# Mask copies and half picks behind each weight rounding in the recurrent heads

## The reference

```python
score = jnp.einsum('bqh,bqhs->bqs', wi, jax.nn.relu(dots)).astype(jnp.float32)
score = jnp.where(causal[None], score, -jnp.inf)
_, idx = lax.top_k(score, topk)
```

```python
A = jnp.einsum('bthk,bshk,btshk->bhts', qc, kc, decay)      # decay = exp(G[t] - G[s]) for s <= t
o_intra = jnp.einsum('bhts,bshv->bthv', A, vc)
new_state = jnp.exp(G_last)[..., None] * state + jnp.einsum('bshk,bshv->bhkv', k_dec, vc)
```

## Time and profile before

| | us |
|---|---|
| timed executions | 3150.56, 3150.81, 3156.08 |
| profiled execution | 3153.85 |
| its span, first to last instruction | 3152.1 |
| the four heads in it (step 0 of head 0 to the norm sum of head 3) | 600.4 to 784.1 |
| mean granted TensorE clock | 0.973 of full |

### The profile page before, as it was taken

The page is one execution under the profiler, slowest core; times in us unless marked ns, Lnnn a source line. Parts: engine busy times, 40 slices in busy tenths (PEclk is TensorE's granted clock), DMA queues, the critical chain, the costliest instruction groups (busy, mean ns, idle before and its releaser), DMA issues.

```text
span 3152.1 us, 37108 instructions
## 1 busy us (share of the span) xinstructions
PE 2947.3 (94%) x12850; PEld 2239.9 (71%) x12858; DVE 1462.5 (46%) x2332; ACT 932.3 (30%) x1629; POOL 1242.4 (39%) x587
## 2 busy tenths in 40 slices
PE   6899998998998999997999899999879999899999
PEld 2688875776665788875766688877657767688787
DVE  7211225887356211237266555524745443455426
ACT  2211003243442211013255233302335551233202
POOL 0455443333134555443422355544321113455544
PEclk9999998999999999998999899999989999999999
DMA  4222231221112222321222122232211112222232
GB/s 157 79 94 93 87 100 62 74 67 55 56 37 87 80 93 93 99 88 60 89 83 64 54 93 94 92 95 93 77 40 37 38 34 74 75 95 95 89 94 98
DMA packets 78617, 249.53 MB, mean 79 GB/s; under 512 B 9073, under 2 KB 15729, under 8 KB 78385
## 3 DMA queue, kind: packets, MB, share of 16 engines
q1 hardware_dynamic: 64800, 229.74, 22.9%
q10 hardware_dynamic: 13712, 18.44, 1.8%
HBM read 238.57 MB, written 9.44 MB: 79 GB/s over the span
## 4 chain that ended last, share of the span: by engine, by line
PE 81%; DVE 10%; ACT 4%; issue 3%; POOL 1%; DMA 1%; ACTq 0%; DVEq 0%; SPq 0%; POOLq 0%
PE ps L300 22%; PE ps L302 22%; PE ps L301 22%; PE ps L3059 1%; PE ps L3102 1%; PE ps L3080 1%; PE ps L3081 1%; DVE tmp L489 1%; DVE tmp L1064 1%; DVE y_ple L1062 1%; PE ps L2582 1%; PE ps L2567 1%; PE ps L1243 1%; PE ps L1876 1%; DVE h L698 1%
## 5 line engine op out<-in xcount | busy, mean ns | idle before, releaser
L294 POOL TENSOR_TENSOR w_lo<-raw,w_hi 128x1024 fp32r<-128x1024 f32 (+1 forms) x438 | 1041.9, 2379 | 1703.4 <-DVE w_hi L287 1703.4
L300 PE MATMUL ps<-xh,w_hi 128*128 128x512 f32 x2152 | 880.6, 409 | 49.4 <-DVE xl L481 20.1
L287 DVE CAST w_hi<-raw 128x1024 fp32r<-128x1024 f32 (+1 forms) x438 | 331.7, 758 | 1132.4 <-PE ps L302 1086.1
L301 PE MATMUL ps<-xl,w_hi 128*128 128x512 f32 x2152 | 856.8, 398 | 0.0
L302 PE MATMUL ps<-xh,w_lo 128*128 128x512 f32 x2152 | 856.1, 398 | 0.0
L300 PEld LDWEIGHTS ps<-xh,w_hi 128*128 128x128 f32 x2152 | 407.3, 189 | 185.2 <-issue 49.2
L302 PEld LDWEIGHTS ps<-xh,w_lo 128*128 128x128 f32 x2152 | 407.6, 189 | 100.5
L301 PEld LDWEIGHTS ps<-xl,w_hi 128*128 128x128 f32 x2152 | 408.5, 190 | 98.5 <-issue 6.5
L300 PE MATMUL ps<-ah,w_hi 128*128 128x512 f32 x704 | 279.6, 397 | 6.8 <-POOL w_lo L294 6.8
L302 PE MATMUL ps<-ah,w_lo 128*128 128x512 f32 x704 | 279.3, 397 | 0.0
L301 PE MATMUL ps<-al,w_hi 128*128 128x512 f32 x704 | 279.1, 396 | 0.0
(11 more groups left out here) (396 smaller groups left out, 3896.7 us busy)
## 6 DMA issues: line engine op xcount, KB each, us to landing
raw<-in_ffn_up SPq DMA_DIRECT2D x90, 512.0 KB, 3.7
raw<-in_conv_up SPq DMA_DIRECT2D x88, 512.0 KB, 3.6
raw<-in_ffn_down SPq DMA_DIRECT2D x32, 512.0 KB, 3.5
raw<-in_conv_down SPq DMA_DIRECT2D x32, 512.0 KB, 3.5
raw<-in_merge SPq DMA_DIRECT2D x24, 512.0 KB, 3.6
raw<-in_ple_gate SPq DMA_DIRECT2D x24, 512.0 KB, 3.6
raw<-in_diff SPq DMA_DIRECT2D x24, 512.0 KB, 3.6
raw<-in_mla SPq DMA_DIRECT2D x20, 512.0 KB, 3.6
```

What stands on the lines that cost most here:

```text
L287: dve.tensor_copy(self.w_hi[s][:, 0:n], self.raw[r][:, 0:n]).then_inc(self.sem["slot_hi"], 1)
L294: pool.tensor_tensor(self.w_lo[s][:, 0:n], self.raw[r][:, 0:n], self.w_hi[s][:, 0:n].bitcast(F32), ALU.subtract).then_inc(self.sem["slot_s ...
L300: pe.matmul(out, wh, xh, start=start, stop=False)
L301: pe.matmul(out, wh, xl, start=False, stop=False)
```

## The change

Only the order of VectorE's instructions in the heads changes; every instruction is still there, and the other engines' programs are the same. Where a level has a rounding, its mask copy stands behind the rounding and no longer ahead of it; where it has none, the copy keeps its place. The picks are cut in two (`largest`: the three MAX8; `mark`: the three MATCH_REPLACE8), and the 22 halves are dealt in turn to eight places of a head: behind the mask copies of the levels 0, 2, 3, 4, 5, 6 and 7, and behind the rounding at S. The heads 0 and 1 take 8 halves each and head 2 takes 6; `masks` follows the last.

```diff
@@ -1562,12 +1562,26 @@
             own = self.part(b)[:, b * P:(b + 1) * P]
             dve.tensor_tensor(own, own, k.causal_b, ALU.add).then_inc(k.sem["topk_masked"], 1)
 
+    def half_pick(self, dve, q, part):
+
+        if part == 0:
+            self.largest(dve, q)
+        else:
+            self.mark(dve, q)
+
     def pick(self, dve, q):
+        self.largest(dve, q)
+        self.mark(dve, q)
+
+    def largest(self, dve, q):
         k = self.k
         dve.wait_ge(*(self.on("topk_replace", 3 * q - 1) if q else self.on("topk_masked", 2)))
         k.carry(dve)
         for b in range(1, NB):
             dve.max(k.top8[:, b - 1, :], self.part(b)).then_inc(k.sem["topk_max"], 1)
+
+    def mark(self, dve, q):
+        k = self.k
         dve.wait_ge(*self.on("topk_max", 3 * q + 2))
         k.carry(dve)
         for b in range(1, NB):
@@ -1725,17 +1739,26 @@
         self.scans(dve, 0)
         self.diff(dve, 0, 1)
         k.round_hi(dve, self.w, 0, 15)
+        halves = iter([(q, part) for q in picks for part in range(2)])
+
+        def half_pick():
+            q, part = next(halves, (None, None))
+            if q is not None:
+                self.half_pick(dve, q, part)
+                if (q, part) == (self.PICKS - 1, 1):
+                    self.masks(dve)
+
         for h in range(self.HEADS):
             self.round_at(dve, h, "V")
             self.diff(dve, h, 2)
             self.product(dve, h, 1)
+            self.round_at(dve, h, 0)
             self.a_out(dve, h, 0)
-            self.round_at(dve, h, 0)
+            half_pick()
             for l in range(2, LEVELS + 1):
                 if l < LEVELS:
                     self.diff(dve, h, l + 1)
                 self.product(dve, h, l)
-                self.a_out(dve, h, l - 1)
                 if l == 3:
                     self.to_end(dve, h)
                 if l == 7:
@@ -1743,30 +1766,23 @@
                     self.round_at(dve, h, "KV")
                 else:
                     self.round_at(dve, h, l - 1)
-                if l in (2, 4, 6):
-                    q = next(picks, None)
-                    if q is not None:
-                        self.pick(dve, q)
-                        if q == self.PICKS - 1:
-                            self.masks(dve)
+                self.a_out(dve, h, l - 1)
+                if l >= 3:
+                    half_pick()
             self.carried(dve, h)
             if h + 1 < self.HEADS:
                 self.forget(dve, h + 1)
+            self.round_at(dve, h, LEVELS)
             self.a_out(dve, h, LEVELS)
-            self.round_at(dve, h, LEVELS)
+            half_pick()
             if h + 1 < self.HEADS:
                 self.scans(dve, h + 1)
                 self.diff(dve, h + 1, 1)
             self.round_at(dve, h, "O")
-            if h + 1 < self.HEADS:
-                q = next(picks, None)
-                if q is not None:
-                    self.pick(dve, q)
-                    if q == self.PICKS - 1:
-                        self.masks(dve)
             self.normed_out(dve, h)
             self.round_at(dve, h, "S")
-        assert next(picks, None) is None
+            half_pick()
+        assert next(halves, None) is None
 
     def gpsimd(self, pool):
         k = self.k
```

## The result

| | runs | median, us | lowest to highest |
|---|---|---|---|
| before | 10 | 3154.21 | 3150.56 to 3156.83 |
| changed | 10 | 3160.56 | 3157.84 to 3164.45 |

The ratio is 1.0021, 95% interval 1.0012 to 1.0029: the change costs 6.4 us by the medians, 4 to 9 by the interval. Forecast were +5.9 us, 3158.2 us, slower more likely than not. Of the 2.4 us between 3158.2 and 3160.56, 1.9 are the base: the kernel before came out at 3154.21 over ten runs, where four had given 3152.3.

What follows compares the result with a forecast made beforehand. TensorE, busy in 94% of the span, was taken as the bound, so its waits decide. The terms 3.7 + 2.2 - 0.5 + 0.5 = +5.9 us on 3152.3 gave 3158.2 us, range 3152 to 3163.

Steps and rivals of the forecast that it cites:

- Part 1: Heads 0 to 2: roundings followed by copies and halves; levels 2, 4 late 1.09, level 6 0.77; gains 0.58 us a head.
- Part 2: Step 7 of heads 0 to 2: the level 7 mask copy behind its rounding delays the output, 1.80 us a head.
- Part 3: Heads 1 and 2: GpSimd's output_low holds VectorE's subtractions, so level 4 starts 1.10 us later, twice: +2.2 us.
- Part 4: Head 3: level 1 waits less, -0.5 us; blocked first subtractions at levels 4 and 6 cost +0.5 us.
- The rival in which VectorE keeps the ports: Heads 1 and 2: VectorE keeps the shared ports, output_low never gets between; +3.7 us in all, chance 0.22.
- The clock: Head 3's level 1 may lose its clock fall, -1.5 us; waits at level 4 and output may bring up to +4.5.
- 14.8 us is about all the stage could ever give back: In the four heads, level matmuls wait for VectorE's hx 12 times, 14.8 us, taken as about the stage's whole possible gain.

Runs made afterwards that it cites:

- copies-ahead kernel: Changed kernel with all mask copies ahead of the roundings, only the picks in halves; +1.8 us, ratio 1.0007 against the kernel before.
- level 7 copy first: Changed kernel with the mask copy of level 7 ahead of its rounding again; +5.1 us, ratio 1.0015 against the kernel before.
- level 7 copy only: Kernel before with only the mask copy of level 7 moved behind its rounding, whole picks kept; +4.9 us, ratio 1.0016 against the kernel before.
- the first experiment: Changed kernel with the level 7 mask copy back ahead of the rounding at step 7; +5.1 us, ratio 1.0015 against the kernel before.
- the last two kernels: Changed kernel, level 7 copy ahead of its rounding, every level prepared one level ahead, output_low later or kept; 3136.72 and 3138.41 us, ratios 0.9944 and 0.9947 against before.

## Why the prediction was right

**Head by head.** From step 0 of one head to step 0 of the next, the kernel before takes 48.44, 48.43 and 45.65 us and the changed one 49.66, 50.70 and 47.92: +1.22, +2.27 and +2.27. Parts 1 to 3 have 1.80 - 0.58 = 1.22 for head 0 and 1.22 + 1.10 = 2.32 for the heads 1 and 2. From step 0 of head 3 to the logits it is 46.95 and 45.33; with the fall of the clock in the first put at 1.6, nothing is left, as part 4 has it. So the terms came one by one, not only their sum.

**Part 1, the roundings followed by copies and halves: right.** The waits came as worked out, 0.94 at level 2, 0.95 at level 4 of head 0, 0.61 to 0.63 at level 6, none at levels 3 and 5. The copies-ahead kernel shows that behind a rounding with a half GpSimd's `w_lo` alone sets the time of the next subtractions.

**Part 2, the level 7 copy: right.** 1.49, 1.49 and 1.50 us of wait; alone it costs 4.8 to 4.9 us, where 3 x 1.80 less 0.5 was worked out.

**Part 3, output_low: right.** 2.02 at level 4 in heads 1 and 2 against 0.95 in head 0, gone when it is moved. The rival in which VectorE keeps the ports fell: the `w_lo` of the earlier trace rows that took 3.51 has no like in the changed kernel, where those in the heads take 2.35 to 2.52. Why four VectorE instructions went ahead of GpSimd in that row stays open; I made no run on it. All six such rows of the kernel before (3.51 or 3.52) stand behind roundings at steps 2 and 4 that had not waited for TensorE, but the rounding at S in the earlier trace rows (743.23) had not waited either and its `w_lo` took 2.46, so that alone is not it. The rule of the Trainium skill that the prediction cites ("SBUF — State Buffer", the section on the two separate sides: an exclusive lock) agrees with the changed kernel's rows, where the two subtractions took 0.66 and 1.48 beside GpSimd's two instructions; it does not account for the six rows of 3.51.

**Part 4, head 3: right.** Its level 1 waits 3.02 for 3.51, its levels 4 and 6 wait 0.94 and 1.68 for 0.71 and 1.46, as worked out. ScalarE shows what lies behind the 3.02. Before, the norm's step (L1432) stood behind the next head's decay (L1394), which waited for VectorE's subtraction; in the changed kernel the decay is done early and the norm's step waits for TensorE's sum:

```profile
739.93 0.63 ACT L1394 ACTIVATE hdiff<-hdiff 128x512 f32<-128x512 f32 x1 [3.14 <-DVE hdiff L1625]
740.47 0.67 ACT L1432 ACTIVATE sq<-ps,consts 128x512 f32<-128x512 f32 x1
```

```profile
743.10 0.63 ACT L1394 ACTIVATE hdiff<-hdiff 128x512 f32<-128x512 f32 x1 [1.33 <-DVE hdiff L1639]
744.82 0.69 ACT L1432 ACTIVATE sq<-ps,consts 128x512 f32<-128x512 f32 x1 [1.08 <-PE ps L1281]
```

So the first part of the output's lateness is taken up by a path that ended later anyway, and the rest goes on to the norm, the rounding at S and level 1. In the experiments level 1 waits 3.0 even where the level 7 copy is ahead of its rounding. There the output of head 2 still waits 0.25 or 1.38, because the key masks now stand ahead of the copy. With 0.25, the first of the two paths still ends last: from level 7 of head 2 to level 1 of head 3 "level 7 copy first" takes 19.52 us, to the hundredth what the kernel before takes, so that wait of 0.25 costs nothing and only moves TensorE's idle time. With 1.5 it takes 20.78, in the changed kernel as in "level 7 copy only". I had left out that wait when I expected 3.5 in the first experiment.

**The clock.** In the profile the fall behind the 3.5 us wait is gone: level 1 to level 2 takes 755.72 - 751.94 = 3.78 where the earlier trace rows have 5.36. So the stage grew by 4.1 only, 5.7 with the fall put back. By the counts above this trace is the exception: behind the same wait of 3.0 the clock fell in the five other kernels that have it, and behind half of the waits of 2.0. An estimate from these counts for an average execution is 5.7 - 1.6 for the fall of before, + 1.3 for level 1 of head 3, + 1.6 for the two places at level 4: +7.0, beside the timed +6.4 with its 4 to 9. I gave the two directions the same weight and left the clock out of the sum. That the sum lies within half a microsecond of the timed median is therefore in part luck; the clock's share can't be told from so few traces.

**What was off** is the base (1.9 us), read from four executions, and the remark that 14.8 us is about all the stage could ever give back. The last two kernels shorten it by 17.6 and 18.8: a fall of the clock went with the waits, and a wait costs more than its idle time (level 2 of the earlier trace rows is idle for 0.71, starts 0.88 late and costs 0.99).

## What to carry to other kernels

On an in-order engine, ask of each instruction moved behind a wait who needs it and when that wait ends: a mask copy behind a rounding that waits for the matmuls just ahead of the copy's own reader is late by the whole rounding and copy, here 1.5 us of wait in each of three heads. Where one engine holds up another's instructions, as GpSimd does VectorE's subtractions here, filling the held time with other work is no gain if the held instruction is the one on the path. Have it done before the other engine is set going: in the last two kernels the subtractions are still held, and TensorE's waits for `hx` are gone.

## What I had not expected of the hardware

- Equal waits of 2.0 us on TensorE brought a fall of the clock in one execution (0.63 over 666 to 670) and none in another (1.00 over the same place of the head), and in "copies ahead" one of each in the same execution. Each fall costs 1.5 to 1.6 us, as much as the waits that one moves about here, so a saving in waits can be hard to see in the median while the trace shows it.
- VectorE's instructions with one SBUF input can be held by GpSimd too: three TENSOR_SCALAR on the scores took 2.03 beside L1799 and 0.89 without it. In the rows shown here MAX8, MATCH_REPLACE8 and the masked copy from PSUM were not held: three MAX8 took 1.47 behind a rounding and 1.46 in the earlier trace rows, MATCH_REPLACE8 0.67 and the copy 0.74 beside GpSimd's 662.56 to 664.98.
